# Gate, up and down projections as seven block products in place of eight, down in a second pass, and the copies of the sliding-window state on another queue

## The reference

```python
def _conv_ffn(xn, conv_state, w_gate, w_up, conv_w, conv_b, w_down):
    g = xn @ w_gate                       # (1088, 1024) x (1024, 2816)
    u = xn @ w_up
    gp = jnp.concatenate([conv_state, g], axis=1)
    gc = conv_b + sum(conv_w[j] * gp[:, j:j + T] for j in range(3))
    y = (jax.nn.silu(gc) * u) @ w_down    # (1088, 2816) x (2816, 1024)
    return y, gp[:, -2:]
```

## Time and profile before

| | us |
|---|---|
| median of 3 runs | 1790.83 (1786.58 to 1793.28) |
| the profiled execution's own time | 1785.58 |
| its span in the profile | 1783.4, granted PE clock 0.98 |
| PE busy | 1701.5 (95%) |
| PEld busy | 1485.6 (83%) |
| DVE busy | 863.5 (48%) |
| ACT busy | 661.8 (37%) |
| POOL busy | 578.4 (32%) |

### The profile page before, as it was taken

The page is one execution under the profiler, slowest core; times in us unless marked ns, Lnnn a source line. Parts: engine busy times, 40 slices in busy tenths (PEclk is TensorE's granted clock), DMA queues, the critical chain, the costliest instruction groups (busy, mean ns, idle before and its releaser), DMA issues.

```text
span 1783.4 us, 27781 instructions
## 1 busy us (share of the span) xinstructions
PE 1701.5 (95%) x9857; PEld 1485.6 (83%) x9857; DVE 863.5 (48%) x1828; ACT 661.8 (37%) x1331; POOL 578.4 (32%) x531
## 2 busy tenths in 40 slices
PE   7999979999997999999899999999999999999996
PEld 6788868888886888888788989888888898888885
DVE  6433335677675776767434332433433324334235
ACT  5222135667675666665322312212112121121113
POOL 0000004566561867778301312212213122121121
PEclk9999977999998999999999999999999999999998
DMA  8232243233306565755612668586595875865912
GB/s 286 101 106 91 97 125 103 70 79 97 80 15 169 166 180 159 186 161 162 224 49 51 137 140 134 132 170 110 117 166 120 155 127 130 163 122 119 154 43 105
DMA packets 156062, 227.46 MB, mean 128 GB/s; under 512 B 31063, under 2 KB 128984, under 8 KB 149528
## 3 DMA queue, kind: packets, MB, share of 16 engines
q1 hardware_dynamic: 153086, 159.39, 30.2%
q0 software_dynamic: 2880, 66.85, 23.0%
HBM read 201.12 MB, written 91.93 MB: 164 GB/s over the span
## 4 chain that ended last, share of the span: by engine, by line
PE 48%; DMA 1%; DVE 1%; ACT 1%; POOL 0%; issue 0%; SPq 0%; ACTq 0%; DVEq 0%; POOLq 0%
PE wide L2646 22%; PE turn L2668 14%; PE rest L2647 7%; PE wide L2321 4%; DMA o_work<-scratch_s_o 1%; PE wide L2744 1%; DMA out_y_prompt<-f_gc 0%; DMA acc<-in_w_gate 0%; PE turn L2333 0%; ACT f_gc L2551 0%; DVE f_gc L2615 0%; PE rest L2653 0%; DVE acc L2570 0%; POOL f_gl L2723 0%; ACT f_rows L2558 0%; POOL f_st L2479 0%
## 5 line engine op out<-in xcount | busy, mean ns | idle before, releaser
L2668 PE MATMUL turn<-lead,f_ah 128*128 128x512 f32 x792 | 240.6, 394 | 5.4 <-DVE f_al L2603 4.0
L2570 DVE TENSOR_TENSOR acc<-turn,acc 128x512 f32<-128x512 f32 x198 | 136.6, 691 | 189.8 <-PE turn L2668 189.8
L2646 PE MATMUL wide<-hT_h,lead 128*128 128x512 f32 x704 | 184.9, 354 | 0.0
L2668 PEld LDWEIGHTS turn<-lead,f_ah 128*128 128x128 f32 x792 | 147.9, 189 | 39.9 <-DVE acc L2570 5.9
L2441 POOL TENSOR_TENSOR f_gl<-f_graw,f_gh 128x1024 fp32r<-128x1024 f32 x21 | 50.6, 2409 | 364.2 <-ACT f_gh L2486 364.2
L1099 POOL TENSOR_SCALAR a_pr<-a_pr,a_rden 128x256 f32<-128x256 f32 (+7 forms) x128 | 94.0, 746 | 188.8 <-DVE a_rden L1199 184.1
L2584 DVE SCALAR_TENSOR_TENSOR f_gc<-wide,f_coef,f_gc 128x832 f32<-128x832 f32 x44 | 47.7, 1085 | 208.0 <-ACT f_lasts L2506 205.1
L2668 PE MATMUL turn<-lead,f_al 128*128 128x512 f32 x352 | 137.2, 390 | 0.0
L804 PE MATMUL zp<-win_h,xT_h 128*128 128x512 f32 (+1 forms) x288 | 112.8, 392 | 3.3 <-DVE acc L655 3.3
L804 PE MATMUL zp<-win_l,xT_h 128*128 128x512 f32 (+1 forms) x288 | 111.3, 387 | 0.0
L2646 PEld LDWEIGHTS wide<-hT_h,lead 128*128 128x128 f32 x704 | 107.6, 188 | 0.0
(11 more groups left out here) (368 smaller groups left out, 4417.1 us busy)
## 6 DMA issues: line engine op xcount, KB each, us to landing
out_s_win_k<-in_state_win_k POOLq DMA_DIRECT2D x10, 3264.0 KB, 43.2
out_s_win_v<-in_state_win_v POOLq DMA_DIRECT2D x10, 3264.0 KB, 45.7
acc<-in_state_win_k SPq DMA_DIRECT2D x16, 768.0 KB, 6.2
acc<-in_state_win_v SPq DMA_DIRECT2D x16, 768.0 KB, 5.7
f_uraw<-in_w_up SPq DMA_DIRECT2D x22, 512.0 KB, 4.6
f_draw<-in_w_down SPq DMA_DIRECT2D x11, 1024.0 KB, 34.1
f_graw<-in_w_gate SPq DMA_DIRECT2D x21, 512.0 KB, 8.2
acc<-in_cache_kv_latent SPq DMA_DIRECT2D x128, 64.0 KB, 1.8
```

Source lines behind the costliest of these rows:

```text
L2570: nc.vector.tensor_tensor(a, dp[h][:], a, ALU.add).then_inc(S["d_add"], 1)
L2646: nc.tensor.matmul(out[:, c0:c1], w[n][:, k, :], x[:, k, c0:c1], start=s, stop=e)
L2668: last = nc.tensor.matmul(dp[h][:], a[:, c, t * P:(t + 1) * P], w[:, c, h * 512:(h + 1) * 512], start=(c == 0 and j == 0), stop=(c == 1 an ...
```

## The change

Gate and up become one product of 2 x 2 blocks: the tokens in two halves of 544 (`a11`, `a12` the first, `a21`, `a22` the second half, each split over the 1024 inputs), the weights of block `f` in four (`b11`, `b21` gate, `b12`, `b22` up). By Winograd's form of Strassen's scheme seven products are made, with sums of token blocks (`s1` to `s4`, made once, by DVE, POOL and ACT, at the start) and of weight blocks (`t1` to `t3`, `n4`, made by POOL for every `f`), and DVE puts the results together (`second`, `fourth`, `up_first`, `up_second`, `gate_second`). A product is 4 slices x 3 terms x 2 pieces of 272 columns. Every operand of the weights has one buffer. The gated result is no longer kept on chip: SP stores it to `s_a` (544 KB and, for the difference of its halves, 256 KB a block), and `h` to `s_h`.

Down becomes a pass of its own behind the last `f`: 7 products x 11 steps, 12 matmuls of 512 columns a step for the prompt, and two more for the sample tokens in the steps of `p1`, `p2`, `p5` and `p3`. A step needs the gated result (one or two pieces of 256 KB from `s_a`, high part by ACT, low part and sum of two by DVE) and a half of `w_down` (loaded once, in 11 loads of 1 MB into the place of the token blocks when these come free; high part by ACT, low part by POOL, and in `p5`, `p6`, `p7`, `p4` POOL first makes a difference of two blocks in place). Four slots each hold steps ahead. DVE adds a product's four banks to one to four places of `acc`, which is loaded back from `s_h`.

The state copies leave POOL: 20 moves of four DMAs each on ACT's queue, 8 requests x 51 rows of 2 KB, every second row, 816 KB. Five stand in `project` (behind tiles 2 to 6), three in the output projection, twelve in the pass over `f` (f = 2, 4, 5, 7, 9, 10, 12, 14, 15, 17, 19, 20), behind `gate_first`. At the end squares and scaling work in halves of 512.

```diff
@@ -43,7 +43,8 @@
 PAGES = PAST // PAGE
 PAIRS = HEADS // 2
 FC = D_FF // P
-MOVES = FC // 2 - 1
+MOVES = 20
+CHUNK = (PAST - DEC_T) // MOVES
...
+def move(eng, io, first, rows):
+    for src, dst in (("state_win_k", "s_win_k"), ("state_win_v", "s_win_v")):
+        a = io[src][:, bass.ds(first + DEC_T, rows), :].rearrange("b (r s) c -> s b r c", s=2)
+        b = io[dst][:, bass.ds(first, rows), :].rearrange("b (r s) c -> s b r c", s=2)
+        for s in range(2):
+            eng.dma_start(b[s], a[s]).then_inc(io["moved"], 16)
...
+                if not isinstance(t.n, int) or t.n == 6:
+                    move(act, io, (t.n - 2) * CHUNK, CHUNK)
...
+DOWN = ("p1", "p2", "p5", "p3", "p6", "p7", "p4")
+STEPS = [(p, j) for p in DOWN for j in range(HF)]
+TARGETS = {"p1": ((0, 0), (0, 1), (4, 0), (4, 1)), "p2": ((0, 0),), "p5": ((0, 1), (4, 1)), "p3": ((0, 1),),
+           "p6": ((0, 1), (4, 0), (4, 1)), "p7": ((4, 0), (4, 1)), "p4": ((4, 0),)}
+ACTS = {"p1": ((0, 0),), "p2": ((0, HF),), "p5": ((1, 0), (1, HF)), "p3": ((2, HF), (2, 0)), "p6": ((1, HF), (2, 0)),
+        "p7": ((2, 0),), "p4": ((1, HF),)}
+SLOTS = 4
...
+PRODUCTS = (("p1", "p2", "p4", "p5", "p6", "p7", "p3"), ("p1", "p6", "p2", "p7", "p5", "p4", "p3"))
...
+        R, Q, V, Z = (ps(n) for n in ("r_ps", "q_ps", "v_ps", "z_ps"))
...
+        turning = [bank(R, 0), bank(R, 1), bank(Q, 0), bank(Q, 1), bank(V, 1), bank(Z, 0), bank(Z, 1)]
...
+            def store_a(f):
+                sp.wait_ge(S["act"], 2 * f + 1)
+                sp.dma_start(s_a[f, :, 0:TOK], us[:]).then_inc(S["a_st"], 16)
+                sp.wait_ge(S["act"], 2 * f + 2)
+                sp.dma_start(s_a[f, :, TOK:A_COLS], diff).then_inc(S["d_st"], 16)
...
+            def load_piece(m):
+                n = step_of[m]
+                p, j = STEPS[n]
+                kind, at = ACTS[p][m - piece_of[n].start]
+                if m >= 10:
+                    sp.wait_ge(S["a_lo"], step_of[m - 6] + 1)
+                if m >= 5:
+                    sp.wait_ge(*a_in(m - 5))
+                c = (0, SEQ // 2, TOK)[kind]
+                sp.dma_start(piece(m), s_a[j + at, :, c:c + 512]).then_inc(S[f"a_in{m % 5}"], 16)
+            def load_w(q):
+                if q >= 4:
+                    sp.wait_ge(*w_in(2 * q - 8))
+                sp.dma_start(wd[q][:, 0:2 * D_MODEL].rearrange("p (f n) -> p f n", f=2),
+                             io["w_down"].rearrange("(f p) n -> p f n", p=P)[:, 2 * q:2 * q + 2, :]).then_inc(S[f"w_in{q % 4}"], 16)
+            def load_h(a, b):
+                sp.dma_start(acc[:, a:b, :], s_h[a:b].rearrange("t p n -> p t n")).then_inc(S["h_in"], 16)
...
+            for f in range(FC):
+                if f + 2 < FC:
+                    sp.wait_ge(S["lo"], 7 * f + 7)
+                    load_raw("g", f + 2)
+                    load_raw("u", f + 2)
...
+            for q, free in ((0, "p1"), (1, "p1"), (2, "p6"), (3, "p6"), (4, "p2"), (5, "p2"), (6, "p7"), (7, "p7"),
+                            (8, "p5"), (9, "p5"), (10, "p4")):
+                sp.wait_ge(S["product"], MADE[free, FC - 1])
+                if q == 10:
+                    for m in range(4, 8):
+                        load_piece(m)
+                load_w(q)
+            store_a(FC - 1)
+            sp.wait_ge(S["a_st"], 16 * FC)
+            load_piece(8)
...
+            load_piece(15)
+            sp.wait_ge(S["rows_out"], 32)
+            load_h(4, PT)
...
+            def combine(f):
+                b = halves(f)
+                pool.wait_ge(*raw_in(f))
+                if f:
+                    pool.wait_ge(S["lo"], 7 * f)
+                nc.gpsimd.tensor_tensor(T["t3"], b["b22"], b["b12"], ALU.subtract).then_inc(S["t_f"], 1)
+                pool.wait_ge(S["t_f"], 4 * f + 1)
+                nc.gpsimd.tensor_tensor(T["t2"], T["t3"], b["b11"], ALU.add).then_inc(S["t_f"], 1)
+                nc.gpsimd.tensor_tensor(T["t1"], b["b12"], b["b11"], ALU.subtract).then_inc(S["t_f"], 1)
+                pool.wait_ge(S["t_f"], 4 * f + 2)
+                nc.gpsimd.tensor_tensor(T["n4"], b["b21"], T["t2"], ALU.subtract).then_inc(S["t_f"], 1)
...
+            for f in range(1, FC):
+                combine(f)
+                b = halves(f)
+                for n in ORDERS[min(f, 2)]:
+                    low(n, b[n], f)
...
+                w = w_half(row + j, h)
+                if p in ("p5", "p6", "p7", "p4"):
+                    pool.wait_ge(*w_in(j))
+                    pool.wait_ge(*w_in(j + HF))
+                    if p == "p5":
+                        a, c = w_half(j, 1), w_half(j, 0)
...
+                    nc.gpsimd.tensor_tensor(w, a, c, ALU.subtract).then_inc(S["t_sum"], 1)
+                pool.wait_ge(S["b_hi"], n + 1)
+                nc.gpsimd.tensor_tensor(ob[n % SLOTS][:, 1, :], w, ob[n % SLOTS][:, 0, :].bitcast(F32), ALU.subtract)\
+                    .then_inc(S["b_lo"], 1)
...
+            def high_a(n):
+                p, j = STEPS[n]
+                if n >= SLOTS:
+                    act.wait_ge(S["step"], n - SLOTS + 1)
+                elif oa_free[n]:
+                    act.wait_ge(S["product"], MADE[oa_free[n], FC - 1])
+                m = piece_of[n][0]
+                if len(ACTS[p]) == 2:
+                    act.wait_ge(S["a_sum"], sums(n + 1))
+                else:
+                    act.wait_ge(*a_in(m))
+                copy(oa[n % SLOTS][:, 0, :], piece(m)).then_inc(S["a_hi"], 1)
+            def high_b(n):
+                p, j = STEPS[n]
+                row, h = down_w[p]
+                if n < SLOTS:
+                    act.wait_ge(S["product"], MADE[ob_free[n], FC - 1])
+                if p in ("p5", "p6", "p7", "p4"):
+                    act.wait_ge(S["t_sum"], t_sums(n + 1))
+                else:
+                    act.wait_ge(*w_in(row + j))
+                copy(ob[n % SLOTS][:, 0, :], w_half(row + j, h)).then_inc(S["b_hi"], 1)
...
+            moving = [f for f in range(1, FC - 1) if f * 3 % 5 < 3]
...
+            for f in range(1, FC):
+                more = f + 1 < FC
+                gate_silu(f - 1)
+                keep_p1(f)
+                if more:
+                    high("b11", f + 1)
+                    high("t2", f + 1)
+                else:
+                    high_a(0)
+                    sample_high(0)
+                gate_first(f)
+                if f in moving:
+                    move(act, io, (8 + moving.index(f)) * CHUNK, CHUNK)
...
+            def fourth(f):
+                dve.wait_ge(S["product"], MADE["p7", f])
+                if f:
+                    dve.wait_ge(S["d_st"], 16 * f)
+                tt(cols(u3), pair(Q), cols(x1), ALU.add).then_inc(S["u"], 1)
+            def up_second(f):
+                dve.wait_ge(S["product"], MADE["p5", f])
+                dve.wait_ge(S["u"], 2 * f + 2)
+                if f:
+                    dve.wait_ge(S["a_st"], 16 * f)
+                tt(cols(us[:, HALF:]), pair(Z), cols(u3), ALU.add).then_inc(S["quad"], 1)
...
+            def low_a(n):
+                p, j = STEPS[n]
+                first, k = piece(piece_of[n][0]), piece_of[n]
+                if len(k) == 2:
+                    for m in k:
+                        dve.wait_ge(*a_in(m))
+                    tt(first, first, piece(k[1]), ALU.subtract if p == "p6" else ALU.add).then_inc(S["a_sum"], 1)
+                dve.wait_ge(S["a_hi"], n + 1)
+                less(oa[n % SLOTS][:, 1, :], first, oa[n % SLOTS][:, 0, :]).then_inc(S["a_lo"], 1)
...
+                if n == 13:
+                    dve.wait_ge(S["h_in"], 80)
+                if 0 <= i < len(DOWN) - 1 and k < 4:
+                    add(i, k)
...
+            def product(f, region, x, w, start):
+                pe.wait_ge(S["lo"], SPLIT_AT[w, f])
+                for k in range(HC):
+                    for i, (a, b) in enumerate(((0, 0), (0, 1), (1, 0))):
+                        for c in range(2):
+                            last = nc.tensor.matmul(region[:, c * 512:c * 512 + PIECE], op[w][:, a, k * P:(k + 1) * P],
+                                                    X[x][b][:, k, c * PIECE:(c + 1) * PIECE], start=start and k == 0 and i == 0,
+                                                    stop=k == HC - 1 and i == 2, skip_group_check=not start)
...
+            for f in range(1, FC):
+                pe.wait_ge(S["tap"], 4 * f - 2)
+                product(f, R, "a11", "b11", True)
+                pe.wait_ge(S["u"], 2 * f)
+                product(f, Q, "s2", "t2", True)
+                pe.wait_ge(S["x1"], f + 1)
+                product(f, R, "a12", "b21", False)
+                pe.wait_ge(S["u"], 2 * f + 1)
+                product(f, Q, "s3", "t3", False)
+                pe.wait_ge(S["quad"], 3 * f)
+                product(f, Z, "s1", "t1", True)
+                pe.wait_ge(S["quad"], 3 * f - 1)
+                product(f, V, "a22", "n4", True)
+                pe.wait_ge(S["quad"], 3 * f + 1)
```

(15 more changed lines are left out.)

1323 lines of the change are left out of this document (790 added, 533 removed).

## The result

The changed kernel takes **1854.66 us** (median of 4 runs, 1851.61 to 1857.11) against 1789.53 us before: ratio **1.036**, 95% interval 1.034 to 1.039. It is slower by 65 us, where I forecast 25 less; 1854.66 lies above my range as well.

A forecast was written before the change was run, and what follows sets the result against it. PE was taken as the bound: 1785.6 us less 60.1 without copies gives 1725.5, plus 34.5 for the copies 1760.0; with the profiled execution 5.2 us under the median, forecast 1765, range 1712 to 1840.

The forecast's parts named there:

- Gate and up: Blocks f: 168 matmuls of 272 columns at 0.127 us, 21.3 us a block, 59.3 us less in all.
- 272 columns at the pace of 320: Gate and up, rival: 272 columns take 0.147 us, 74 us more, 1840; chance 0.03.
- The state copies: Copies on ACT's queue: 14.5 us more in project, nothing in the output projection, 20 in the blocks; 34.5 together.
- eight engines become the bound: Project and blocks, rival: DVE behind stores, ACT behind its DMAs; 1841 at 0.125 us a row; chance 0.22.
- The other rival for the copies: State copies cost nothing, as the queue takes a whole move or sixteen engines carry it: median 1731; chance 0.27.
- Block 0: Making s1 to s4 first: p3 ends 29.4 us after the last output product, 6.6 us more.
- Down: Pass behind the blocks: fewer matmuls 30.1 us less, old waits 8.6 less, new waits 21 and 14 more.
- The step in turn: Down, p5, p6, p7, p4: POOL and ACT alternate, 3.44 us a step, 21 us more together.
- VectorE holds up GpSimd: Down, rival: POOL waits for DVE's two-input SBUF operations, some 25 us more, median 1790; chance 0.10.
- The end: Behind the last matmul: 10.5 us in place of 14.3, 3.7 us less.
- ACT's issues take under 1 us: State copies, sign that the forecast is wrong: each DMA issue on ACT takes under 1 us.
- PE waits in single blocks too: Blocks, sign that the forecast is wrong: PE waits also in blocks that don't follow two moves.

The follow-up runs named there:

- experiments 3 and 5: Both against the changed kernel: 3, copies with rows outermost (90 and 12 in place of 8), 1778.92 us; 5, K and V of a copy issued apart, 1837.87 us.
- experiment 11: Block 0's two `recombine` sums moved from GpSimd to VectorE, on top of the kernel where VectorE makes down's 44 differences: 1740.43 us, ratio 0.974.
- the version on VectorE: Down's 44 differences moved from GpSimd to VectorE, 11 steps ahead, on top of the 1753.28 us kernel with VectorE's sums one step ahead: 1739.52 us.

## Why the prediction was wrong, step by step

I gave 1765 and "faster" 0.66; it is slower. Of the 90 us between forecast and result 50 are the copies, for a reason that I had among the rivals but priced too low; the other 40 are in the main block 0 and down.

- **Gate and up: right.** 24 matmuls of 272 columns take 3.01 us, 0.1255 each (I took 0.127), and 21.15 us a block. The rival "272 columns at the pace of 320" is out: 5.81 us for 24 came only at 1.2 GHz.
- **The state copies: the step that failed.** Forecast 34.5 us, measured 84.3. The parts of the mechanism stand: eight engines, a queue that takes only so many rows an engine, rows at 0.110 x 16 x 1855.3 / 33280 = 0.098 us (I took 0.094; the 0.204 of my upper bound came from packets of 52,224 bytes, not from rows). What failed is the price of standing. I let 80 rows an engine drain at 0.094 as if the engines had nothing else, 7.5 us. In project only 58 to 62 rows an engine had gone when the fourth issue ended (so some 148 wait, not 128), but these took 9 to 10.8 us, 0.15 to 0.19 each, and the first of them began 1.5 to 2.6 us behind the first issue. ScalarE sat idle for 9.4 to 12.7 us there and for 7.6 to 12.4 in the blocks. That it is the loads and stores on the same engines that double the price fits the rows, but no run takes them away. In *project* I gave 2.9 us a tile; on the average of the five it is 4.8 of wait and 2.1 of longer busy time at the lower clock: 34.3 in place of 14.5. In *the output projection* I counted only ScalarE's work and said "nothing"; the load of a tile shares the eight engines and lands after a median of 10.6 us in place of 3.8, and ScalarE's standing lies on the chain too: 10.4. In *the blocks* I said that a single copy costs nothing and a pair 5; the late ScalarE and the slower store add up, singles cost 7.6 together, pairs 27 and the last block 3, 37.1 in all in place of 20. The rival "eight engines become the bound" decides, as I wrote, from about 0.11 us a row; the row in itself stayed under that, but what a row costs with others between them did not (0.15 to 0.19). That it was eight engines, and ScalarE behind its own DMAs, is what experiments 3 and 5 show.
- **The other rival for the copies**, that they cost nothing, had 1731 as its time. The kernel without copies takes 1770. So even with this step right I would have been 39 us off, in the main in block 0 and in down.
- **Block 0:** forecast 29.4 us behind the last output product, measured 44.0 without copies. PE is busy 30.5 of 44 us at a granted clock of 0.81. I had 6.6 of waits and find 13.5. I scaled each engine's rate from instructions that ran alone, and here they are stretched (experiment 11 shows one, 4.77 for 1.28); that this makes the whole difference is not shown. The other 8 are the lower clock, which I did not count anywhere.

```profile
973.00:1017.00 44.00, 30.49 (x186) 29.29 (x185) 40.56 (x28) 19.77 (x32) 33.71 (x19) 0.81 0.12 31
```

- **Down:** forecast 265.7, measured 298.5 without copies. PE's waits sum up to 44.4 against my 35, in other places: 9.0 for `d_x` in p5 (forecast 2.8; VectorE's chain, which I left out), 9.1 at the start (14), 3.0 for the sample add (nothing), 15.8 for GpSimd's low parts and 6.8 for adds at the start of p7 and p4, which are gone when the differences are left out (forecast 18.5 for both). The largest, with their causes, here in the changed kernel:

```profile
PE v_ps L3205 <- DVE d_x L2840: 9.5, 9, 1.7
PE q_ps L3214 <- POOL u_op L2552: 4.5, 5, 1.3
PE v_ps L3132 <- ACT acc L2697: 4.4, 1, 4.4
...
PE r_ps L3214 <- DVE acc L2971: 4.0, 1, 4.0
...
PE q_ps L3214 <- DVE acc L2971: 3.7, 1, 3.7
```

  The step in turn is 3.71 us at the end of p6, near my 3.44: the difference takes 1.74 there, where I had 1.29. In p7 it is 4.6 to 4.7, since five of its steps have 1.1 us of roots each, where I had 0.55, and in p4 it is 4.3 with 0.64 of roots, which I left out. The other 23 us are in PE's busy time: 254 us for what I priced at 230.7. The pace of 0.231 is 3 us of it, and the 22 transposes of the last rows, which I forgot, are 3.8; the clock's mean of 0.96 accounts for some 12 (an estimate, 0.04 x 299); the rest I cannot split. With the waits go most of both: in the version on VectorE down takes 260, PE is busy for 244.
- **VectorE holds up GpSimd:** I gave it 0.10 as a rival and 25 us. It was no alternative but a part of every case, and it works in both directions. My argument against it was the gap while ScalarE casts. In p6 VectorE's low part and its sum run into GpSimd's difference, which takes 1.74 for 1.28; and where the gap was taken out, one VectorE instruction took 14.58 us.
- **The end:** 10.5 forecast, 9.4 measured. Right.
- Of my signs: "ACT's issues take under 1 us" did not come, "PE waits in single blocks too" did.

## What to carry to other kernels

A DMA issue is work of its engine once its queue is full, and here the queue filled per DMA engine: before moving a copy anywhere else, put a dimension outermost that spreads it over many engines (90 over fifteen here, in place of 8 over eight); another order of the dimensions gave 76 of 84 us. Price a stall by what else uses the same engines at the time, and add the lower clock that PE comes back with. Where GpSimd and VectorE both read SBUF side by side, price them nearer to the sum of their times than to the longer one, give the work to VectorE if it has room, and look for VectorE's longest instruction before you close the gaps in GpSimd's order.

## What I had not expected of the hardware

- Small waits cost more than they last: in project five waits of 24.0 us together cost 34.3, in block 0 13.5 cost 21 (44.0 less 22.8 of work), with a granted clock of 0.90 in the first tiles and of 0.81 in block 0.
- One VectorE instruction of 2.30 us took 14.58 beside eleven GpSimd instructions without a gap, and 9.72 beside seven; each time it ended 1.1 us behind the last of them.
- Packets of 51 KB on GpSimd's queue were free beside loads that had time, and cost 249 us (2019.3 against 1770.3) beside stores in the same queue as those loads.
- An issue took 0.88 us with 90 rows outermost and 0.82 with 12, against 0.68 with 8 batches outermost: it hardly follows the bytes (1440, 192 and 816 KB).
